# Two fused transformer blocks on one core: PSUM tiles copied out raw, two norm squares moved to TensorE, two squares moved up ScalarE's queue

## The reference, cut to what matters

```
x: [1, 512, 1024]
for l in range(2):
    sh1, sc1, gt1, sh2, sc2, gt2 = split(silu(c) @ w_ada[l] + b_ada[l])
    h = rms_norm(x, norm_mix[l]) * (1 + sc1) + sh1
    dn_qkv, dn_z, dn_a, dn_b, sw_q, sw_k, sw_v, gate_a, gate_b = split(h @ w_in[l])
    dn_qkv = silu(causal_dwconv(dn_qkv, dn_conv[l]))      # 24 tiles of 128 channels
    dq, dk = l2_norm(dq), l2_norm(dk)                      # 16 tiles, one per head
    o_dn = gated_delta_rule(dq, dk, dv, g, beta)
    o_dn = rms_norm(o_dn, dn_norm[l]) * silu(dn_z)         # 8 tiles
    y_a = o_dn @ w_dn_out[l];  y_b = window_attention(...) @ w_swa_out[l]
    x = x + gt1 * ((sigmoid(gate_a) * y_a + sigmoid(gate_b) * y_b) @ w_o[l])
    h = rms_norm(x, norm_ffn[l]) * (1 + sc2) + sh2
    up_act, up_lin = split(h @ w_up[l])
    x = x + gt2 * ((silu(causal_dwconv(up_act)) * up_lin) @ w_down[l])
second block: h = rms_norm(x); attention, a state space layer, gates; final rms_norm
```

## Time and profile before

| What | Value |
|---|---|
| median of three runs | 2664.87 us (2664.43 to 2666.22) |
| profiled execution | 2667.91 us, span 2666.1 us, mean granted TensorE clock 0.972 |
| TensorE matmuls busy | 2528.7 us, 95% |
| VectorE busy | 1451.2 us, 54% |
| ScalarE busy | 1084.1 us, 41% |
| GpSimd busy | 1043.4 us, 39% |

### The profile page before, as it was taken

One profiled execution on the slowest core, in us unless ns is written; L12 is line 12 of the kernel. 1 busy time (PEld: TensorE's weight loads), 2 busy tenths in 40 slices (PEclk: granted clock), 3 DMA queues, 4 the chain that ended last, 5 costly groups with the idle time before them and its releaser, 6 DMA issues. The chain is left out here.

```text
span 2666.1 us, 33330 instructions
## 1 busy us (share of the span) xinstructions
PE 2528.7 (95%) x13145; PEld 2039.1 (76%) x13145; DVE 1451.2 (54%) x2429; ACT 1084.1 (41%) x1904; POOL 1043.4 (39%) x560
## 2 busy tenths in 40 slices
PE   5999999999989999999999999999999998999998
PEld 3777777887868888867777878787888886776787
DVE  6399658654555545646994652363444207836322
ACT  3446663245333332234665523533333223336532
POOL 1556622112434444335664221244444444322342
PEclk8999998999989999999999999999999999999999
DMA  7221426634324426532232252322322335731232
GB/s 245 79 73 55 143 78 173 185 111 146 126 79 142 142 95 215 199 110 72 64 127 80 58 136 81 119 85 77 107 95 95 95 102 140 156 96 40 72 127 78
DMA packets 331391, 299.94 MB, mean 113 GB/s; under 512 B 56718, under 2 KB 302820, under 8 KB 330212
## 3 DMA queue, kind: packets, MB, share of 16 engines
q1 hardware_dynamic: 279268, 279.46, 33.5%
q10 hardware_dynamic: 51968, 18.35, 2.7%
HBM read 267.85 MB, written 29.93 MB: 112 GB/s over the span
## 5 line engine op out<-in xcount | busy, mean ns | idle before, releaser
L217 POOL TENSOR_TENSOR split<-ring,split 128x1024 fp32r<-128x1024 f32 (+2 forms) x340 | 806.8, 2374 | 1234.2 <-ACT split L213 1193.7
L277 PE MATMUL ps<-hh,split 128*128 128x512 f32 x3808 | 1244.7, 401 | 12.3 <-ACT wk L1987 7.1
L277 PEld LDWEIGHTS ps<-hh,split 128*128 128x128 f32 x3808 | 717.7, 189 | 175.2 <-issue 27.9
L277 PE MATMUL ps<-hl,split 128*128 128x512 f32 x1904 | 758.5, 398 | 0.0
L213 ACT ACTIVATE split<-ring 128x1024 fp32r<-128x1024 f32 (+1 forms) x336 | 341.3, 1017 | 855.4 <-PE ps L277 648.2
L277 PEld LDWEIGHTS ps<-hl,split 128*128 128x128 f32 x1904 | 364.1, 191 | 76.1 <-issue 8.4
L277 PE MATMUL ps<-split 128*128 128x512 f32 x1152 | 280.8, 401 | 0.1
L277 PEld LDWEIGHTS ps<-split 128*128 128x128 f32 x1152 | 216.0, 188 | 59.5 <-issue 14.4
L612 POOL TENSOR_TENSOR split<-ring,split 128x1024 fp32r<-128x1024 f32 x32 | 76.5, 2390 | 313.2 <-ACT split L604 313.2
L2281 PE MATMUL ps<-split 128*128 128x512 f32 x704 | 174.4, 401 | 0.0
L2281 PEld LDWEIGHTS ps<-split 128*128 128x128 f32 x704 | 136.3, 195 | 28.8
(11 more groups left out here) (422 smaller groups left out, 3383.4 us busy)
## 6 DMA issues: line engine op xcount, KB each, us to landing
ring<-in_w_in_dram SPq DMA_DIRECT2D x60, 1024.0 KB, 5.2
ring<-in_w_up_dram SPq DMA_DIRECT2D x44, 1024.0 KB, 5.1
ring<-in_w_in_dram SPq DMA_DIRECT2D x34, 512.0 KB, 5.0
big<-in_w_ada_dram SPq DMA_DIRECT2D x16, 1024.0 KB, 8.9
ring<-in_w_ada_dram SPq DMA_DIRECT2D x32, 512.0 KB, 3.6
spare<-in_w_ada_dram SPq DMA_DIRECT2D x16, 1024.0 KB, 7.5
ring<-in_w_down_dram SPq DMA_DIRECT2D x16, 896.0 KB, 5.3
ring<-in_w_swa_out_dram SPq DMA_DIRECT2D x8, 1024.0 KB, 5.2
```

The source lines that it names most:

```text
L217: on.tensor_tensor(halves(pt, nk)[1], slot(n, nk)[:, :, e * P:(e + 1) * P], halves(pt, nk)[0], ALU.subtract).then_inc(low_made, 1)
L277: ins = nc.tensor.matmul(ps[bank[gt]][:, :], w[:, k, :], rhs[e][:, k, :], start=(n == 0), stop=(n == 3 * nk - 1))
```

## The change

Five edits.

1. `first_pair` does its last pass tile by tile: all eight k of the first tile, then all eight of the second.
2. In the q/k/v stage ScalarE squares heads 0 and 1 ahead of the last five silus, behind a wait for the attention's last but one pair of transposes (`a_tp`), whose SBUF home the squares use.
3. In Z, VectorE copies tiles 0 to 3 raw from PSUM into `z`, each behind the scaling of head 2t+1, and frees the bank. ScalarE's silu of these four then works in place in SBUF, and VectorE's product waits for it by `f_silu`.
4. In the feed-forward norm VectorE adds squares 1 to 5 only. TensorE multiplies the sum with ones as soon as that is there, then square 6, then square 7.
5. The same in the norm behind the down projection.

```
                 for group in passes:
-                    for k in range(KD):
-                        for e in range(2):
-                            for a, r in group:
...
+                    by_tile = group is passes[-1]
+                    for n in range(2 * KD):
+                        k, e = (n % KD, n // KD) if by_tile else (n // 2, n % 2)
+                        for a, r in group:
...
                                 for n in range(max(t - SILU, 0), t):
                                     silu(n)
+                        act.wait_ge(a_tp, 2 * doubles - 2)
+                        for n in range(2):
+                            act.wait_ge(silu_made, order[n] + 1)
+                            nc.scalar.activation(wk[:, 8 + n, :], big[:, order[n], :], ACT.Square).then_inc(n_squared, 1)
                         for t in range(QKV_TILES - SILU - 1, QKV_TILES):
                             silu(t)
...
-                        square(0)
-                        square(1)
                         for t in range(KD):
                             root(2 * t)
...
-                        pe.wait_ge(ffn_summed, KD - 2)
+                        pe.wait_ge(ffn_summed, KD - 3)
                         nc.tensor.matmul(ps[7][:, :], ones, square_sum, start=True, stop=False)
-                        pe.wait_ge(ffn_squared, KD)
-                        nc.tensor.matmul(ps[7][:, :], ones, wk[:, 8 + (KD - 1) % 2, :], start=False, stop=True
-                                         ).then_inc(ffn_summed, 2)
+                        for t in range(KD - 2, KD):
+                            pe.wait_ge(ffn_squared, t + 1)
+                            ins = nc.tensor.matmul(ps[7][:, :], ones, wk[:, 8 + t % 2, :], start=False, stop=(t == KD - 1))
+                        ins.then_inc(ffn_summed, 3)
...
                         def silu(t):
                             gt = G_Z + t
+                            if t < 4:
+                                act.wait_ge(evacuated[bank[gt]], use[gt] + 1)
+                                nc.scalar.activation(z[:, t, :], z[:, t, :], ACT.Silu).then_inc(f_silu, 1)
+                                return
...
+                            if h % 2:
+                                gt = G_Z + h // 2
+                                dve.wait_ge(part_made, gt + 1)
+                                nc.vector.tensor_copy(z[:, h // 2, :], ps[bank[gt]][:, :]).then_inc(evacuated[bank[gt]], 1)
                         for t in range(KD + 1):
                             if t < KD:
-                                dve.wait_ge(evacuated[bank[G_Z + t]], use[G_Z + t] + 1)
+                                if t < 4:
+                                    dve.wait_ge(f_silu, t + 1)
+                                else:
+                                    dve.wait_ge(evacuated[bank[G_Z + t]], use[G_Z + t] + 1)
...
-                            if t >= 2:
+                            if 2 <= t < KD - 1:
                                 sum_square(t - 1)
...
-                        pe.wait_ge(mix_summed, KD - 2)
+                        pe.wait_ge(mix_summed, KD - 3)
                         nc.tensor.matmul(ps[7][:, :], ones, mix_sum, start=True, stop=False)
-                        pe.wait_ge(mix_squared, KD)
-                        nc.tensor.matmul(ps[7][:, :], ones, mix_square(KD - 1), start=False, stop=True).then_inc(mix_summed, 2)
+                        for k in range(KD - 2, KD):
+                            pe.wait_ge(mix_squared, k + 1)
+                            ins = nc.tensor.matmul(ps[7][:, :], ones, mix_square(k), start=False, stop=(k == KD - 1))
+                        ins.then_inc(mix_summed, 3)
```

More of the change, by code:

```diff
@@ L291, in first_pair @@
                 for group in passes:
-                    for k in range(KD):
-                        for e in range(2):
-                            for a, r in group:
[L295 to L304, removed]
+                    by_tile = group is passes[-1]
+                    for n in range(2 * KD):
+                        k, e = (n % KD, n // KD) if by_tile else (n // 2, n % 2)
+                        for a, r in group:
+                            if a == 1 and not waited and (e == 1 or not low_of_second):
+                                pe.wait_ge(low_made, gt0 + 2)
+                                waited = True
+                            if a == 0 and e == 0:
+                                pe.wait_ge(made[r], k + 1)
+                            ins = nc.tensor.matmul(ps[bank[gt0 + e]][0:sizes[e], :], weights[e][a][:, k, :], (hh, hl)[r][:, k, :],
+                                                   start=(k == 0 and a == 0 and r == 0),
+                                                   stop=(k == KD - 1 and (a, r) == both[2]))
+                        if k == KD - 1 and both[2] in group:
+                            ins.then_inc(part_made, 1)
             def by_token(bank, whole, n=P):
@@ L993, in build @@
                     silu_made = sem("silu_made")
+                    n_squared, n_summed, n_rs, n_scaled = (sem("n_" + s) for s in ("squared", "summed", "rs", "scaled"))
+                    order = [8 * side + 4 * g + n for g in range(2) for side in range(2) for n in range(4)]
                     o_swa = split[:, SPLIT_WK:SPLIT_WK + KD, :], split[:, SPLIT_SQ:SPLIT_SQ + KD, :]
@@ L1239, in _ @@
                                     silu(n)
+                        act.wait_ge(a_tp, 2 * doubles - 2)
+                        for n in range(2):
+                            act.wait_ge(silu_made, order[n] + 1)
+                            nc.scalar.activation(wk[:, 8 + n, :], big[:, order[n], :], ACT.Square).then_inc(n_squared, 1)
                         for t in range(QKV_TILES - SILU - 1, QKV_TILES):
                             silu(t)
-                    n_squared, n_summed, n_rs, n_scaled = (sem("n_" + s) for s in ("squared", "summed", "rs", "scaled"))
-                    order = [8 * side + 4 * g + n for g in range(2) for side in range(2) for n in range(4)]
                     @block.sync
@@ L1280, in square @@
                         def square(n):
-                            if n >= 2:
-                                act.wait_ge(n_summed, n - 1)
+                            act.wait_ge(n_summed, n - 1)
                             act.wait_ge(silu_made, order[n] + 1)
@@ L2322, in _ @@
                                                                    op0=ALU.mult, op1=ALU.add).then_inc(evacuated[bank[gt]], 1)
-                                    if 4 * i + m >= 2:
+                                    if 2 <= 4 * i + m < KD - 1:
                                         sum_down(dve, 4 * i + m - 1)
```

## The result

The changed kernel takes 2630.6 us (median of 4 runs, 2629.2 to 2631.0) against 2664.65 (4 runs, 2661.2 to 2666.2) of the kernel before on the same chip: ratio 0.9877, 95% interval 0.9865 to 0.9889. The forecast was 2637.3, range 2632 to 2647. The profiled execution took 2630.95 (span 2629.0, granted clock 0.980; before: 2667.91, 2666.1, 0.972).

A forecast was written before the change was run, and what follows sets the result against it. TensorE, 95% busy, was taken to bound the kernel. Terms 6.5 + 11.8 + 5.6 + 2.3 + 1.4 = 27.6 us turn the profiled 2667.91 into 2640.3 and, off the median 2664.87, give 2637.3 us; range 2632 to 2647.

The forecast's parts named there:

- Edit 2, 6.5: q/k/v stage: squares ahead of the last silus remove TensorE's whole gap before the first sum, both layers, 6.5 us.
- Edit 3, 11.8: Z, both layers: gap before tile Z+4 goes, 7.3 us, and slow clock right behind it is returned, 4.5; together 11.8.
- Edit 4, 5.2 - 0.6 + 1.0: Feed-forward norm: Ln earlier by 5.2 us in layer 0 and 1.0 in layer 1, layer 0's following pass 0.6 worse; 5.6.
- The term of -0.6: Pass with hh behind layer 0's feed-forward norm: expected to look as layer 1's does, 0.6 us worse.
- Edit 1, 2.3: Up pairs' pass with hl: by tile, ScalarE's making of the next weights is hidden, 1.13 us, twice: 2.3.
- edit 5, 1.4: Mix norm behind the down projection: Ln 0.7 us earlier, twice: 1.4.
- the rival's 1.6 four times: First pairs: by tile, the first tile waits for the last hl, 1.6 us in four pairs; 2646.0, chance 0.04.
- Table loads: Rival: square isn't in silu's table set, two more loads of 1.28 us a layer; 2639.7, chance 0.03.
- Absorption by modulation weights: Rival: layer 0's gain is absorbed by the next layer's modulation weight loads, 14.3 us lost; 2651.6, chance 0.04.
- A slower clock for a denser TensorE: Rival: a denser TensorE is granted less clock; 138 more matmuls at the lower level lose all; slower than before, chance 0.03.
- The slow clock isn't returned: Rival: low clock falls elsewhere, behind remaining idle times; 4.5 and 1.8 us missing, 21.3 saved, 2643.6, chance 0.13.
- the first rival: The rival "The slow clock isn't returned"; its words: five passes at layer and norm starts stay as they are; chance 0.13.

The follow-up runs named there:

- z_wait_filled: Kernel before, with three products of constants ahead of tile Z+4 in each layer, results unused: 2659.3 us, ratio 0.9981.
- hh_wait_filled: Changed kernel, with three products of constants ahead of the up pair in each layer, results unused: 2630.7 us, ratio 0.9874.
- old_waits_filled: Kernel before, with constant products in waits at Z+4, add of squares, up pair, mix norm and first pair, not at SO's squares: 2654.9 us, ratio 0.9963.
- changed_again: The changed kernel, unaltered, on another chip: 2629.5 us, ratio 0.9861.
- the four delayed ones: Changed kernel with 1, 2, 3 or 4 constant products (0.9 us each) ahead of tile Z+0 in each layer: 2629.8, 2637.4, 2628.4 and 2637.3 us.
- edit 3 alone: Kernel before with only raw copies of Z by VectorE and silu in place: 2642.5 us, ratio 0.9919.

## Why the prediction was right, and where it failed

**Edit 2, 6.5.** Right in every row: sum at once behind the half tile, no second table load, square 2 in time. Alone it gave 7.6.

**Edit 3, 11.8.** The wait of 7.3 is gone, and the 4.5 of slow clock behind it came back with it; `z_wait_filled` shows that the standing still had caused it. All eight copies took 0.68, none behind GpSimd, and delayed nothing. VectorE's line of them (min, median and max in ns, first and last start):

```profile
L2049 DVE COPY wk<-ps x8: 676/678/679, 613.4 to 1698.8; 128x512 f32<-128x512 f32 x8
```

**Edit 4, 5.2 - 0.6 + 1.0.** From the last sum of Z to Ln in layer 0 the changed kernel is 10.4 us shorter (15.8 off at Ln, 5.4 of them by the last sum), and Z's 3.65 + 1.8 of clock and this norm's 5.2 make 10.6. In layer 1 it is 7.2 against 7.5. The term of -0.6 is the one that failed, below.

**Edit 1, 2.3, and edit 5, 1.4.** Both as forecast at their places. From the Ln of layer 0's feed-forward norm to that of its mix norm the kernel is 3.6 us shorter: 1.8 are these two, 2.3 the faster pass with hh, less the 0.3 for hl, which makes 3.8. The wait for hl is real, appears where the pass ahead runs at full clock, and is worth 0.3, not the rival's 1.6 four times.

**The rivals.** Table loads: no. Absorption by modulation weights: no, layer 0's 19.4 us at its end are all there at the program's end. A slower clock for a denser TensorE: no, it lost 15 us less. "The slow clock isn't returned" holds in single places (`hh_wait_filled`, `old_waits_filled`), not for the change as a whole.

**The step that failed** is this one, of edit 4: "The wait for hh stays at 3.07 in both, and the pass behind it is slow in both [...] I expect layer 0 to look as layer 1 does, 0.6 worse", and with it the assumption, in words only under the first rival, that what stands at layer and norm starts stays as it is. The waits did stay. The passes went from 9.78 to 7.52, from 10.46 to 9.20 and from 10.37 to 8.96: 4.9 us off, where I had 0.6 on. With the 0.3 of hl that is 5.2 of the 9.4 us between 2640.3 and the profiled 2630.95. Of the rest some 1.9 lie at the program's start, where the first pass with hh begins at 50.09 instead of 52.06 and no edit has come yet, about 1.0 in the second block, and 1.3 (9.4 - 5.2 - 1.9 - 1.0, rounded) I can't put down to one row. The profiled execution of before was 3.0 above its median, so in medians the miss is 6.7. In `changed_again` the passes took 9.14, 9.53 and 8.92, 3.0 us off in all, and the total is the same: that the passes get shorter holds in both, by how much each does not.

**What stands in its place.** Ahead of the up pairs it is the idle time that brings the slow clock: in the six executions where products fill that wait, all twelve passes with `hh` take 7.50 to 7.54. (At layer 1's start, where the products fill only part of a longer wait, passes of 7.95 to 9.19 remain.) How long it lasts is not fixed by what stands just ahead: the same pass behind the same 3.07 takes 7.5 to 10.4 us in the kernels here, and 7.52 and 9.14 in two executions of one. So a saving ahead of an untouched wait prices the pass behind that wait anew. The profiled execution of before had three passes of about 10 and lost 56.6 us in all.

Slow stretches stand elsewhere too, behind less idle time. Four times in layer 0's down projection the changed kernel loses 1.7 us, 6.8 of its 41.5, and so does the kernel before, each time behind narrow products (128x1) with 0.3 to 0.6 us of idle time among them. In one of the places, 14 matmuls take 5.06 that take 3.33 elsewhere in that stage:

```profile
1051.47 1.05 PE L396 MATMUL ps<-cst,kd 128*128 128x1 f32 x8 [0.60 <-DVE kd L389]
1052.39 5.06 PE L2295 MATMUL ps<-split 128*128 128x512 f32 x14
```

No kernel here tries to mend such a place, so what brings the lower clock there is not shown.

Was the changed kernel lucky, then? In six executions of it without filled waits (the two above and the four delayed ones) it lost 28.7 to 44.5 us, 38.4 on average; before and the six kernels with some of its edits lost 41.9 to 56.6, 49.2 on average. The profiled execution of before is the worst of all of them: its granted clock was 0.972, the mean of the 68 other executions of that kernel, on five chips, 0.9745, while the eight of the changed kernel had 0.980 to 0.982. So of the 15.1 us of clock between the two profiled executions some 10 come with the change, by this estimate from the two averages; I had counted 6.3, and which edit brings the others isn't shown. Some 5 belong to an execution of before that was slower than most. What sets the length of a remaining pass is not visible in these traces. That it is the place in time is no more than a guess: the delayed kernels fit it, but two executions of the changed kernel differ as well. It stays open.

Beside these measurements: the Trainium skill, "TensorE: Matmul & The Clock Gate", What's actually happening, says that how many matmuls run at the lower level, from the kernel's start on, varies between runs of the same kernel. The passes here agree, in the middle of a kernel: the same 32 matmuls of the changed kernel took 7.52 us in one execution and 9.14 in another.

The range failed for the same reason: its lower end, 2632, took single passes at full clock off a sum in which the clock's loss over the whole span stood as if fixed. Its own terms were not all in it either: the two up passes (2.4 and 3.0) alone bring 2637.3 to 2631.9, and the first passes named beside them got nothing. With the numbers since measured (waits 21.9 off, clock 5 to 20 off: the 49.2 above less 44.5 to 28.7) it would have had to reach down to about 2623.

## What to carry to other kernels

Sum the waits that an edit removes from the rows, and book the clock apart: add up busy time times (1 - granted clock) over the whole span, see which of it stands behind waits that go, and give the rest a range of its own, since every wait that stays is priced anew when work ahead of it moves. To compare two kernels at the same clock, fill the waits of both with constant matmuls: here that turned 34 measured us into 23.7 against a forecast of 21.9, but only once the wait for the squares was filled too; with it left out it was 30.1. And where a wait can't be removed, filling it is itself a gain (5 us here for six products a layer).

## What the runs showed of the hardware

- A pass of 32 matmuls behind one and the same wait of 3.07 took 7.5 to 10.4 us, with nothing different just ahead of it; in two executions of one kernel it took 7.52 and 9.14.
- Products of 128x1 with 0.3 to 0.6 us of idle time among them were followed by a loss of 1.7 us to the slow clock, four times in layer 0's down projection (14 matmuls took 5.06 us instead of 3.33).
- A delay of 1.8 us a layer made the kernel 7 us slower, one of 2.7 us no slower.
- One program's executions differ with the clock: the kernel before went from 2656.5 us at a granted clock of 0.977 to 2671.5 at 0.971, over five chips.
- A VectorE add with two SBUF inputs took 2.7 to 2.8 us instead of 0.69, once in ten to twelve. In three kernels it was the add that started 0.13 to 0.19 us behind a GpSimd subtraction; one that started 0.16 ahead of such a subtraction took 0.69 (edit 3 alone). With the adds of layer 0 9 to 11 us earlier it was the fifth instead of the sixth, and in the changed kernel it falls where nobody waits (min, median and max in ns):

```profile
L2081 DVE TENSOR_TENSOR big<-big,wk x10: 691/693/2808, 714.9 to 1800.5; 128x512 f32<-128x512 f32 x10
```
